# One table set for logarithm and exponential on ScalarE in four stages of a hybrid mLSTM, GLA and MoE layer

## The reference, cut to what matters

```python
def rms_norm(x, g):
    xf = x.astype(jnp.float32)
    xf = xf * lax.rsqrt(jnp.mean(xf * xf, axis=-1, keepdims=True) + EPS)
...
def mlstm_scan(q, k, v, i_pre, f_pre, state, with_output):
    log_f = jax.nn.log_sigmoid(f_pre)
        w = jnp.exp(log_w - m_new[..., None])
        decay = jnp.exp(b_end + m - m_new)
...
log_a = jax.nn.log_sigmoid(jnp.einsum('btdr,dre->dbte', lr, gla_w2) + gla_b2) / GLA_TAU
def gla_scan(q, k, v, log_a, state, with_output):
        b = jnp.cumsum(ac, axis=2)
        b_end = b[:, :, -1]
        s_new = jnp.exp(b_end)[..., None] * s_mat + einsum(kc * jnp.exp(b_end[:, :, None] - b), vc)
...
x = x + gt2 * ffn(rms_norm(x, g_norm2[l]) * (1.0 + sc2) + sh2)
return rms_norm(x, g_final)
```

## Time and profile before

| | us |
|---|---|
| time, median of 3 runs (3126.46 to 3147.04) | 3146.8 |
| the profiled execution's own time | 3143.02 |
| its span, from the first to the last instruction | 3141.4 |
| busy in the span: PE | 2514.2 (80%) |
| busy in the span: DVE | 1480.5 (47%) |
| busy in the span: ACT | 954.7 (30%) |
| all ACT_TABLE_LOADs of L1164 and L1177, 20 each | 51.4 |

### The profile page before, as it was taken

The page is one execution under the profiler, slowest core; times in us unless marked ns, Lnnn a source line. Parts: engine busy times, 40 slices in busy tenths (PEclk is TensorE's granted clock), DMA queues, the critical chain, the costliest instruction groups (busy, mean ns, idle before and its releaser), DMA issues. The chain is left out here.

```text
span 3141.4 us, 29863 instructions
## 1 busy us (share of the span) xinstructions
PE 2514.2 (80%) x10662; PEld 1952.5 (62%) x10662; DVE 1480.5 (47%) x1894; ACT 954.7 (30%) x1048; POOL 498.6 (16%) x477
## 2 busy tenths in 40 slices
PE   7649999999799659994676676599982899999980
PEld 1138888887354348883566665477762677777760
DVE  0150101110570144433767777364332788888875
ACT  0231111111000110003333232244221666767755
POOL 4020010100000010001222222112002111111105
PEclk9769999999899857775666666699995899999995
DMA  7352222321311011111000010565532899999965
GB/s 269 126 178 77 101 77 101 102 76 47 107 27 39 5 41 33 47 54 47 21 13 20 13 47 27 175 191 178 171 104 101 319 369 371 377 377 369 378 253 234
DMA packets 238759, 444.53 MB, mean 142 GB/s; under 512 B 19872, under 2 KB 91568, under 8 KB 238430
## 3 DMA queue, kind: packets, MB, share of 16 engines
q1 hardware_dynamic: 218156, 373.23, 33.9%
q0 software_dynamic: 15632, 51.94, 4.5%
q10 hardware_dynamic: 4900, 18.41, 1.4%
HBM read 371.69 MB, written 71.85 MB: 141 GB/s over the span
## 5 line engine op out<-in xcount | busy, mean ns | idle before, releaser
L2178 DVE TENSOR_TENSOR ex_w_lo<-ex_raw,ex_w_hi 128x2048 fp32r<-128x2048 f32 x186 | 417.8, 2288 | 111.9 <-ACT ex_w_hi L2138 110.5
L2138 ACT ACTIVATE ex_w_hi<-ex_raw 128x2048 fp32r<-128x2048 f32 x186 | 345.9, 1908 | 92.0 <-DMA ex_raw<-in_w_up_dram 57.1
L448 PE MATMUL qk_ps<-h_t,qk_w 128*128 128x512 f32 (+1 forms) x640 | 249.2, 552 | 25.2 <-DMA h_t<-h_kept 23.4
L664 DVE CAST rows_w_hi<-rows_w 128x2048 fp32r<-128x2048 f32 x24 | 29.4, 1223 | 417.4 <-PE rows_ps L651 404.7
L681 ACT ACTIVATE rows_stage<-rows_ps 128x512 f32<-128x512 f32 x104 | 62.2, 599 | 512.9 <-PE rows_ps L651 512.9
L448 PEld LDWEIGHTS qk_ps<-h_t,qk_w 128*128 128x128 f32 x640 | 122.0, 191 | 152.4 <-issue 149.2
L649 PE MATMUL rows_ps<-h_hi,rows_w_hi 128*128 128x512 f32 x512 | 199.2, 389 | 0.0
L650 PE MATMUL rows_ps<-h_lo,rows_w_hi 128*128 128x512 f32 x512 | 199.2, 389 | 0.0
L651 PE MATMUL rows_ps<-h_hi,rows_w_lo 128*128 128x512 f32 x512 | 199.2, 389 | 0.0
L1248 PEld LDWEIGHTS gl_lv_ps<-gl_q_level,gl_k_level 128*128 128x128 f32 x896 | 159.0, 273 | 5.2 <-issue 3.4
L1248 PE MATMUL gl_lv_ps<-gl_q_level,gl_k_level 128*128 128x64 f32 x896 | 159.4, 356 | 0.0
(11 more groups left out here) (337 smaller groups left out, 5484.8 us busy)
## 6 DMA issues: line engine op xcount, KB each, us to landing
ex_raw<-in_w_up_dram SPq DMA_DIRECT2D x62, 2048.0 KB, 12.7
ex_raw<-in_w_down_dram SPq DMA_DIRECT2D x31, 2048.0 KB, 9.8
mod_w<-in_w_mod_dram SPq DMA_DIRECT2D x12, 2048.0 KB, 9.1
rows_w<-in_w_in_dram SPq DMA_DIRECT2D x24, 1024.0 KB, 6.2
out_gates<-rows_stage POOLq DMA_DIRECT2D x64, 256.0 KB, 2.3
expert_rows<-ex_y ACTq DMA_DIRECT2D x31, 512.0 KB, 7.6
vals<-rows_stage POOLq DMA_DIRECT2D x40, 256.0 KB, 2.3
ml_v<-vals SPq DMA_DIRECT2D x20, 512.0 KB, 3.3
```

Of the source, the lines that this page charges most:

```text
L448: last = pe.matmul(ps[j][:, at:at + n], wt[:, j, k, :], m.h_t[:, k, t0:t0 + n], start=(k == 0), stop=(k == KD - 1))
L2138: act.activation(hi[:, q, h], raw[:, q, h], ACT.Copy).then_inc(hi_done[q], 1)
L2178: dve.tensor_tensor(lo[:, q, at], raw[:, q, at], hi[:, q, at].bitcast(F32), ALU.subtract)\
```

## The change

ACT's list in each of the four stages begins with a load of the set that holds both functions.

```diff
@@ norm_in
         def _(act):
+            act.preload_act_table_set('natural_log_exp_and_others')
             def normalise(i):
```

## The result

The changed kernel takes 3128.26 us in the median (20 runs, 3092.62 to 3140.53), the kernel before 3146.7 (20 runs, 3120.41 to 3154.36). That is 18.4 us less; 17.1 less, and a time of 3129.7, were forecast. The profiled execution took 3130.38, its span 3128.7.

What follows compares the result with a forecast made beforehand. Most of the loads' 84 us was taken to run beside other work. gla_scan 5.2, norm_in 7.7, gate_rows 1.3 and combine 2.9 make 17.1 off 3143.0, 3125.9; plus 3.8 for the median, 3129.7 (range 3106 to 3147).

Steps and rivals of the forecast that it cites:

- the rival without queue and port: norm_in and combine: load and store don't meet, addition isn't held up; 23.9 us saved, 3122.9 us; chance 0.13.
- loads cost twice their row: All four stages: ACTIVATEs beside a load hide as much again; 34.2 us saved, 3112.6 us; chance 0.02.
- every load counts: All four stages: all 65 removed loads save 1.29 us each, 84 us in all, 3063 us; chance 0.02.
- the term: gla_scan: four of L1164's loads shorten the chain at 1.29 us each, 5.2 us saved; bounds 3.9 to 6.5.
- Pairs 0, 1 and 3: norm_in: these three pairs save 2.58 us each, 7.7 us in all; bounds 5.2 to 12.9.
- The step that said the load's data wait for the data of a store ahead: norm_in: a load of x issued behind a store is 0.66 us late and queues 1.9, losing the 2.6 gained.
- One sign: norm_in: periods alternating between about 8.2 and 10.7 us, with a store right ahead of the load in the short ones.
- Start: combine's start: the fourth addition ends about 1.1 us after POOL, at 3103.7 rather than 3104.72; 1.0 us saved.
- End: combine's end: the last product no longer waits 1.95 us for the last norm; 1.95 us saved.
- Body: combine's body: DVE is never idle and ACT runs beside it, so 12 of the loads save nothing.
- The clock in the mLSTM scan: mLSTM scan: earlier start changes TensorE's clock; all chunks long gives 3156.5 us, all short 3107.3; chance 0.10 each.
- the low way: mLSTM scan: all 15 chunks stay in the long form, 26.8 us more, kernel at 3156.5 us; chance 0.10.

Runs made afterwards that it cites:

- the first experiment: Changed kernel with norm_in's store of pair i-2 moved behind the load of pair i: norm_in 55.96 us against 59.86 in the changed kernel.
- the loads put back: Changed kernel without the set load at the start of gate_rows and gla_scan: gate_rows 40.71 us (+1.27), gla_scan 560.75 us (+4.97).
- the cut product: Changed kernel with POOL's gate product in combine cut to one of 1024 columns: combine 53.28 us, 3.53 a tile.
- the further version: Changed kernel, norm_in's store held until x has landed, combine's gate product on DVE, not POOL: 3095.28 us (0.9916 of before); later 3123.10 (0.9913).

## Why the prediction was right

The interval of the times, 13 to 29 us, would also hold the 23.9 of the rival without queue and port; what bears the prediction out are the stages.

**The price of a load** was 1.29 us: 1.27 in `gate_rows`, 1.24 in `gla_scan` when the loads were put back. That loads cost twice their row falls with it, and so does the case in which every load counts.

**gla_scan.** Of the four gaps between logarithms that were to give 1.29, three gave 1.28 each; the first gap gave nothing, and chunks with an output are as long as before, as forecast. The fourth of them, the fifth gap, fell from 24.04 to 20.44, so the term was 1.7 too small in the profile after. Stretches of that gap (columns as in the earlier trace rows) in the kernel before,

```profile
1487.28:1511.32 24.04, 11.84 (x47) 10.33 (x47) 17.31 (x32) 9.71 (x10) 7.80 (x9) 0.57 0.07 22
```

in the changed kernel,

```profile
1478.37:1498.81 20.44, 9.52 (x50) 8.16 (x50) 17.32 (x32) 7.14 (x7) 7.80 (x9) 0.67 0.08 26
```

and in the first experiment, whose `gla_scan` is the same code:

```profile
1479.22:1501.99 22.77, 11.85 (x47) 10.33 (x47) 17.32 (x32) 7.14 (x8) 7.81 (x9) 0.50 0.07 23
```

In the first experiment PE is busy as long as before (11.85 and 11.84), at a granted clock of 0.50, the lower of the two levels (1.2 of 2.4 GHz) throughout; 22.77 is 24.04 less 1.27. With that chunk `gla_scan` takes 557.35, that is 5.31 less than before, and the forecast said 5.2. In the changed kernel the clock is 0.67 and PE is busy 2.3 less: this is the rest of the gap, and it is not ACT's time. Six of the ten profiles with the set in `norm_in` have the faster chunk (the 21.64 of the loads put back is one of them), and none of the three without; whether the earlier start brings it is open.

**norm_in.** Pairs 0, 1 and 3 were to give 2.58 each, and 2 and 4 nothing. Up to the first copies the stage is 2.44 shorter, and its four periods are 1.97, 0.06, 2.59 and 0.55 shorter: 7.61 in all, 7.00 of it in the three pairs that were counted. The parts were right, then, and not by luck only their sum; the short periods are 8.62 and 8.48 rather than 8.2, as Square waits longer for x. The first edit showed that the store is the cause of most of what pairs 2 and 4 lost. The step that said the load's data wait for the data of a store ahead was too simple, since a store behind a load can slow it as well; here the two pictures give the same sum. One sign was worded the wrong way round: the store stands right ahead of the load in the long periods, as the working had it, and not in the short ones.

**combine.** Start: from the stage's start to the end of the fourth addition it is 1.69 less, of which 0.66 are there at the first addition already, ahead of any norm; the remaining 1.03 stand against a forecast of 1.0. The addition ends 1.08 after POOL's product, forecast 1.1. End: from the start of the last residual to the end of the last product it is 2.03 less, against 1.95. Body: nothing, as forecast, with the reason that the cut product confirmed. That two single profiles match to 0.1 is in part luck: three with the loads have 69.32 to 70.37 in this stage and five without 66.43 to 67.53, which is 3.0 less in the mean and 1.8 to 3.9 by pairs.

**The rivals.** No queue and no port: the alternation and the 2.81 of the addition speak against it. The clock in the mLSTM scan: the long chunks (17.4) did begin one chunk earlier, and the stage was 4.75 longer, in the direction of the low way, but it is 299 to 305 in the other profiles, with either set of loads. What the prediction did not see is that the larger place of that kind is `gla_scan` (below). The median stayed in the middle of its range; that of the single runs (3092.62 to 3140.53) reaches below it.

## What to carry to other kernels

Count the loads, then price only those at whose end someone waits: of 65 some 14 were paid for (17.8 / 1.29, with the 5.31 of `gla_scan`). Ask at each what comes late next; here it was a store close to a load, and a DVE that POOL kept busy. With POOL's product out of the way the same change was worth 12.5 and 7.8 in `combine` instead of 3.64. Naming the set that holds both functions made none of the four stages longer, and it paid more where less other work hid the loads.

## What the hardware showed that was not expected

The same `gla_scan` runs at two speeds within one execution. Stretches of one chunk each, of the further version:

```profile
1600.00:1630.70 30.70, 21.37 (x102) 19.50 (x101) 22.43 (x40) 7.15 (x7) 7.51 (x9) 0.67 0.05 17
1727.30:1754.60 27.30, 18.04 (x100) 16.45 (x100) 22.35 (x41) 7.15 (x7) 7.45 (x9) 0.81 0.06 20
```

With nearly the same instructions, PE is busy for 21.37 at a granted clock of 0.67 (a mean of stretches at 1.2 and at 2.4 GHz) and for 18.04 at 0.81. In that execution the stage took 523.59, in the second profile of the same kernel, on another chip, 555.64: 32 us that no line of the code explains, more than the change is worth. In the chunk at 1660, shortly ahead of the rise, PE was busy for the same 21.37 of 30.70, at 0.75; what sets it off is open. The runs as a whole follow the clock too: the changed kernel's fastest of 3092.62 has a mean of 0.866, the profiled one of 3130.38 has 0.852. The kernel before has this spread too: on the chip of the further version's first runs it took from 3105.17, at 0.867, to 3158.09, at 0.848. These runs have no profile, so in which stage the clock rose in them isn't shown. A gain of 17 us in this kernel can be seen in medians and in stage lengths, not in a single run.
